# Reordered splits, forms and late T forms in a pooling-mixer and SwiGLU kernel on one core

## What is computed

```python
h = concat(meta, x)                        # 16 + 2048 rows
u = h @ w_in                               # 4 groups of 256 features
d = trailing_mean(u, window) - u           # windows 2, 4, 8, 16, one per group
y = (d @ w_group) * scale                  # 256 x 256 per group
h = layer_norm(ALPHA * h + y @ w_out, g1, b1)
gate, up = split(h @ w_gu)                 # 2816 features each
h = layer_norm(ALPHA * h + (silu(gate) * up) @ w_down, g2, b2)
out = h[16:]
```

## Time and profile before

| | us |
|---|---|
| median of 3 runs (lowest, highest) | 1678.73 (1674.95, 1679.14) |
| the profiled execution | 1677.85 |
| its span | 1676.1 |
| TensorE busy | 1648.3 |
| VectorE busy | 1056.1 |
| GpSimd busy | 707.4 |
| ScalarE busy | 616.5 |

### The profile page before, as it was taken

How to read it: one execution, slowest core, us unless ns; L and a number is a source line. 1 busy time by engine, 2 the same in 40 slices (tenths; PEclk the granted TensorE clock), 3 DMA queues, 4 the chain that set the end, 5 groups by cost and what they waited for, 6 DMA issues and landing times.

```text
span 1676.1 us, 19060 instructions
## 1 busy us (share of the span) xinstructions
PE 1648.3 (98%) x7314; PEld 1360.7 (81%) x7314; DVE 1056.1 (63%) x1069; ACT 616.5 (37%) x836; POOL 707.4 (42%) x455
## 2 busy tenths in 40 slices
PE   9999999999999999999999999999999999999998
PEld 7777888787888888888888887788888888888886
DVE  6679876897444444344757678777654443468866
ACT  5234455355433333434533333333343322232320
POOL 0336125604455566565366777676632000341002
PEclk9999999999999999999999999999999999999999
DMA  9574377544445455466556778775658443554542
GB/s 342 215 273 164 113 262 281 199 162 151 163 151 164 157 195 195 153 226 229 188 181 204 221 245 252 262 219 176 210 179 306 159 156 128 193 211 173 198 149 93
DMA packets 190953, 330.83 MB, mean 197 GB/s; under 512 B 8464, under 2 KB 132496, under 8 KB 181136
## 3 DMA queue, kind: packets, MB, share of 16 engines
q1 hardware_dynamic: 151168, 297.64, 51.4%
q10 hardware_dynamic: 37520, 23.60, 4.7%
q0 software_dynamic: 2176, 8.39, 1.3%
HBM read 227.36 MB, written 102.24 MB: 197 GB/s over the span
## 4 chain that ended last, share of the span: by engine, by line
PE 81%; DVE 5%; POOL 5%; DMA 4%; issue 2%; ACT 1%; SPq 1%; POOLq 0%; DVEq 0%; ACTq 0%
PE acc L1241 37%; PE acc L1270 19%; PE turn L1241 6%; PE turn L1270 6%; PE acc L1108 5%; PE acc L1074 5%; PE turn L1108 3%; DVE sums L1708 2%; DMA wr<-w_gu 1%; POOL ss_mix L871 1%; POOL wt L871 1%; DVE split L1663 1%; DMA hf_dram<-ss_mix 1%; PE acc L1138 1%; POOL dt_t L871 1%
## 5 line engine op out<-in xcount | busy, mean ns | idle before, releaser
L1241 PE MATMUL acc<-fa,wf 128*128 128x512 f32 x1584 | 367.9, 392 | 3.3 <-ACT acc L1586 3.3
L1241 PE MATMUL acc<-fb,wf 128*128 128x512 f32 x1584 | 364.6, 390 | 3.6 <-DVE acc L1930 3.1
L1241 PEld LDWEIGHTS acc<-fb,wf 128*128 128x128 f32 x1584 | 296.8, 188 | 67.6 <-DVE wf L1815 4.0
L1241 PEld LDWEIGHTS acc<-fa,wf 128*128 128x128 f32 x1584 | 297.1, 189 | 65.5 <-issue 4.1
L1270 PE MATMUL acc<-dw,da 128*128 128x512 f32 x1386 | 315.3, 389 | 0.0
L1270 PEld LDWEIGHTS acc<-dw,da 128*128 128x128 f32 x1386 | 260.3, 188 | 53.9
L1815 DVE TENSOR_TENSOR wf<-wt,wf 128x512 fp32r<-128x512 f32 x132 | 136.3, 1037 | 150.7 <-ACT wf L1442 150.2
L1815 DVE TENSOR_TENSOR wf<-wr,wf 128x512 fp32r<-128x512 f32 x176 | 181.8, 1037 | 54.4 <-ACT wf L1442 54.0
L871 POOL TENSOR_TENSOR wt<-wr,wt 128x512 f32<-128x512 f32 x88 | 131.5, 1494 | 163.8 <-DVE wf L1815 163.5
L1074 PE MATMUL acc<-mov,split 128*128 128x512 f32 x768 | 180.4, 394 | 5.8 <-DVE split L1663 5.8
L1442 ACT CAST wf<-wr 128x512 fp32r<-128x512 f32 x176 | 108.7, 618 | 207.9 <-PE acc L1241 205.6
(11 more groups left out here) (136 smaller groups left out, 1963.1 us busy)
## 6 DMA issues: line engine op xcount, KB each, us to landing
wr<-w_gu SPq DMA_DIRECT2D x44, 1024.0 KB, 5.1
dar<-af_dram SPq DMA_DIRECT2D x56, 704.0 KB, 4.2
af_dram<-g ACTq DMA_DIRECT2D x32, 512.0 KB, 6.7
raw<-w_in SPq DMA_DIRECT2D x15, 1024.0 KB, 6.8
fs<-hf_dram SPq DMA_DIRECT2D x14, 1024.0 KB, 5.7
dt_raw<-w_down SPq DMA_DIRECT2D x22, 512.0 KB, 6.5
wt_dram<-dt_t SPq DMA_DIRECT2D x22, 512.0 KB, 4.2
sa<-af_dram SPq DMA_DIRECT2D x22, 512.0 KB, 7.7
```

The lines of the kernel that those rows point to most:

```text
L1241: mm = nc.tensor.matmul(dst, wf[:, slot, a, k, :], fa[half][i][:, v, :, k, :], start=i < 2 and k == 0 and n3 == 0, stop=k == KC - 1 and n3 ...
```

## The change

- Splits of weight chunks (`split_hi`, `split_lo`) move ahead of `stage_u`, `pool` and `rows_stats` in `mixer_block` and `mixer_products`, on both engines.
- Form 2 of h is split one product sooner (t = 3, not 4); form 4's low part and unit 0's first four splits move ahead of the statistics at t = 6; the last form of half 0 moves from place 0 of unit 0 to places 3 (high) and 4 (low). SP's loads of these forms move ahead accordingly, the last one ahead of four stores of rows.
- The five late T forms move from units 26 to 30 to units 38 to 42.
- The load of `gb` moves from unit 33 to step 8 of the down stage (`MT = 8`), and the wait for it to its first use.
- The products with zeros go from 10 to 14.

```diff
--- before.py
+++ after.py
@@ -409,16 +409,17 @@
 
 
 
-        FORM_HI = {(0, 0): NP - 1, (HALF_UNITS - 4, 3): NP, (HALF_UNITS - 2, 3): NP + 1}
+        FORM_HI = {(0, 3): NP - 1, (HALF_UNITS - 4, 3): NP, (HALF_UNITS - 2, 3): NP + 1}
         FORM_HI.update({(HALF_UNITS - 1, place): NP + q for place, q in ((1, 2), (3, 3), (5, 4), (6, 5))})
         FORM_LO = dict(FORM_HI)
+        FORM_LO[0, 4] = FORM_LO.pop((0, 3))
         FORM_HI.update({(HALF_UNITS, 2): NP + 6})
         FORM_LO.update({(HALF_UNITS, 3): NP + 6})
 
 
         TF_STEPS = 2 * JF
         TF_FIRST = tuple(range(3, HALF_UNITS - 2))
-        TF_UNITS = TF_FIRST + tuple(range(HALF_UNITS + 4, HALF_UNITS + 9))
+        TF_UNITS = TF_FIRST + tuple(range(UNITS - 6, UNITS - 1))
         TF_STEP = {n: step for step, n in enumerate(TF_UNITS)}
         assert len(TF_UNITS) == TF_STEPS
 
@@ -767,18 +768,18 @@
             load_form(0)
             load_form(1)
             load_mix(1, 3)
+            load_form(2)
             load_mix(1, 4)
-            load_form(2)
+            load_form(3)
             load_mix(1, 5)
-            load_form(3)
             load_mix(1, 6)
             load_form(4)
             load_unit(0)
             load_form(5)
             load_unit(1)
+            load_form(6)
             for j in range(TT):
                 store_h(2, j)
-            load_form(6)
 
             for n in range(UNITS):
                 half, jj = n // HALF_UNITS, n // 2
@@ -797,10 +798,6 @@
                     store_tform(TF_STEP[n - 1])
                 if n in TF_STEP:
                     load_tform(TF_STEP[n])
-                if n == TF_UNITS[-1] + 3:
-                    sp.wait_ge(tf_stored, 16 * TF_STEPS)
-                    for q, v in enumerate((ffn_g, ffn_b)):
-                        sp.dma_start(gb[:, q, :], v.partition_broadcast(P)).then_inc(gb_landed, 16)
                 if turned_in(n + 1)[1] == 0:
                     load_pair(turned_in(n + 1)[0])
                 if n == TURN0 + 3 * TT:
@@ -844,6 +841,11 @@
                     load_da(k + 3)
                 if k == 2:
                     store_s(JF - 1)
+                if k == MT:
+
+                    sp.wait_ge(tf_stored, 16 * TF_STEPS)
+                    for q, v in enumerate((ffn_g, ffn_b)):
+                        sp.dma_start(gb[:, q, :], v.partition_broadcast(P)).then_inc(gb_landed, 16)
                 if k < 2:
                     load_hz(k + 2)
                 elif 3 <= k < 7:
@@ -1112,7 +1114,7 @@
 
 
             pe.wait_ge(idle_zero, 1)
-            for _ in range(10):
+            for _ in range(14):
                 nc.tensor.matmul(turn[:, 1, :], idle[:, 0:P], idle[:], start=True, stop=True)
 
             def fold_pair_free(q):
@@ -1451,15 +1453,15 @@
 
             def mixer_block(b):
                 for i in range(PAIRS):
+                    c = c_in(b, i) + 1
+                    if c != c_in(0, 1):
+                        split_hi(c, c % 2)
                     if i >= 1:
                         stage_u(b, i - 1)
                     elif b % 2:
                         stage_u(b - 1, PAIRS - 1)
                     if b == 0:
                         stage_meta(i)
-                    c = c_in(b, i) + 1
-                    if c != c_in(0, 1):
-                        split_hi(c, c % 2)
                     if b == 2 and i >= 2:
                         take_turn(i - 2, 2)
                         take_turn(i - 2, 3)
@@ -1485,17 +1487,17 @@
 
             def mixer_products(h):
                 for t in range(NP):
-                    if t == 0:
-                        stage_u(2 * h + 1, PAIRS - 1)
                     c = c_mix(h, t) + 1
                     if c < MIX_END:
                         split_hi(c, c % 2)
+                    if t == 0:
+                        stage_u(2 * h + 1, PAIRS - 1)
                     if 1 <= t < NP - 1:
                         d_hi(h, t + 1)
                     if h == 0 and t in (0, 1, 2, 4):
                         x_hi(2, (0, 1, 2, 4).index(t))
                     if h:
-                        for q in ((), (0,), (1,), (), (2,), (3,), ())[t]:
+                        for q in ((), (0,), (1,), (2,), (), (3,), ())[t]:
                             form_hi(q)
                     if t == 0:
                         for m in range(TT):
@@ -1817,9 +1819,13 @@
 
             def mixer_block(b):
                 for i in range(PAIRS):
+                    c = c_in(b, i) + 1
+                    if c != c_in(0, 1):
+                        split_lo(c, c % 2)
                     if b == 2 and i == 0:
                         rows_stats(0, 6)
                         stats_are_done(1)
+                        aggregate(1)
                     if b == 0 and i >= 1:
                         take_meta(i - 1)
                         dve.wait_ge(meta_u_taken, i)
@@ -1833,11 +1839,6 @@
                         pool(b, i - 1)
                     elif b % 2:
                         pool(b - 1, PAIRS - 1)
-                    c = c_in(b, i) + 1
-                    if c != c_in(0, 1):
-                        split_lo(c, c % 2)
-                    if b == 2 and i == 0:
-                        aggregate(1)
                     if b % 2 and i in (1, 2):
                         d_lo(b // 2, i - 1)
                     if b in (0, 2):
@@ -1845,28 +1846,27 @@
 
             def mixer_products(h):
                 for t in range(NP):
+                    c = c_mix(h, t) + 1
+                    if c < MIX_END:
+                        split_lo(c, c % 2)
                     if t == 0:
                         pool(2 * h + 1, PAIRS - 1)
-                    if t in (2, 5):
+                    if 1 <= t < NP - 1:
+                        d_lo(h, t + 1)
+                    if h and t == NP - 1:
+                        form_lo(4)
+                        for q in range(4):
+                            unit_lo(0, q)
+                    if t in (2, 5, 6):
                         rows_stats(h, t - 1)
-                    if t == 6:
-                        rows_stats(h, 5)
                     if t == 5:
                         stats_are_done(2 * h)
                         aggregate(2 * h)
-                    c = c_mix(h, t) + 1
-                    if c < MIX_END:
-                        split_lo(c, c % 2)
-                    if 1 <= t < NP - 1:
-                        d_lo(h, t + 1)
                     if h == 0 and t in (0, 1, 2, 4):
                         x_lo(2, (0, 1, 2, 4).index(t))
                     if h:
-                        for q in ((), (0,), (1,), (), (2,), (3,), (4,))[t]:
+                        for q in ((), (0,), (1,), (2,), (), (3,), ())[t]:
                             form_lo(q)
-                    if h and t == NP - 1:
-                        for q in range(4):
-                            unit_lo(0, q)
                     if t in (1, 3, 4, 5, 6):
                         add_rows(h, t)
                     if h and t == NP - 1:
@@ -1931,7 +1931,6 @@
                 if n == 0:
                     unit_lo(0, 5)
                     unit_lo(0, 6)
-                    new_form(0, 0)
                 elif nxt:
                     new_form(n, 3)
                     unit_lo(n + 1, 3)
@@ -1991,7 +1990,6 @@
                         down_w_lo(v)
             dve.wait_ge(prod_done, NP * UNITS)
             up_out(2 * JF - 1, 1, bank(UP_LAST, 1))
-            dve.wait_ge(gb_landed, 32)
             dve.wait_ge(normed, BLOCKS * TT)
 
             def take(k):
@@ -2030,6 +2028,8 @@
                 nc.vector.tensor_scalar(var_eps[:, r:r + 1], mv[:, r, 1:2], EPS, None, ALU.add).then_inc(var_ready, 1)
 
             def row_apply(r, zz):
+                if r == 0:
+                    dve.wait_ge(gb_landed, 32)
                 zz = zz.rearrange("p h t -> p (h t)")
                 nc.vector.scalar_tensor_tensor(out=zz, in0=zz, scalar=mv[:, r, 0:1], in1=gb[:, 0, :],
                                                op0=ALU.subtract, op1=ALU.mult).then_inc(centered, 1)
```

## The result

The change makes the kernel slower: 1684.85 us median of five runs (1683.17 to 1687.53) against 1676.52 us of the kernel before in the same session (1674.95 to 1679.14). The ratio is 1.0048, 95% interval [1.0033, 1.0063]. The forecast was 1671. The profiled execution took 1683.17 us with a span of 1681.4, so it is 5.3 us longer by the profiles and 8.3 us by the medians (that of before was 1.3 us over its new median, that of after is the lowest of its five).

What follows compares the result with a forecast made beforehand. TensorE, busy 98% of the span, was taken as the bound, losing only idle and low-clock time. From 1677.85 us, -1.2 - 5.0 - 2.0 - 5.1 + 2.5 - 2.9 - 3.4 + 10 = -7.1 gave 1671, range 1660 to 1678.

Steps and rivals of the forecast that it cites:

- T forms: Late units: leaving units 26 to 30 wins 3.4 us; units 38 to 42 delay w_down's loads, +10 (+2 to +22).
- What is late next: Third product of each half: later pooling delays GpSimd's sums and the form; +1.5 and +1.0, together +2.5 us.
- Warm-up: Kernel start: four more products with zeros raise the clock for the fold; -1.2 us, ends 0 and -2.6.
- Splits first in the blocks: Blocks 0, 1 and 3: splits ahead of staging and pooling remove TensorE's waits; -5.0, -2.0 and -5.1 us.
- The second rival: Blocks to third products: VectorE's equal work swallows the front's gain, 5 of 12.1 us left, near 1677; chance 0.15.
- Statistics behind the split, last form behind the seed: End of half 1 and unit 0: later statistics cost, the seed's wait goes; -2.9 us, ends -4.1 and 0.
- The +0.8 for unit 0: Unit 0: later aggregate delays GpSimd's weight forms and the first units' splits; +0.8 us, ends 0 and 3.
- The late chain: Unit 42 to first down step: last T form's stores and loads hold SP's queue, stored 40.0 us after unit start.
- The slower rival: First down step: SP's queue starves w_down's loads by more, +22 to +26 us, time about 1684; chance 0.13.

Runs made afterwards that it cites:

- the last form alone: Kernel before with only the last form of h cast and split behind unit 0's seed, its load ahead of four stores; 1673.39 us, ratio 0.9986.
- the one a unit sooner: Kernel after with its last five T forms in units 37 to 41 instead of 38 to 42; 1679.07 us, ratio 1.0011.
- the best of after: Kernel after with T forms in units 27, 29, 31, 33, 35, statistics again ahead of the products' splits, GpSimd's sums reordered; 1670.02 us, ratio 0.9962.
- the one with odd units: Kernel after with the last five T forms in units 27, 29, 31, 33 and 35 instead of 38 to 42; 1677.70 us, ratio 1.0009.

## Why the prediction was wrong

By TensorE's timeline, the forecast for everything up to unit 1 was -13.7 us and the trace shows -2.2; for the T forms it was +6.6 and the trace shows +7.5. The step that failed is "What is late next": the loss at the third products, put at +2.5, is +12.7.

**Warm-up:** the meta products start 1.35 us sooner, forecast 1.2. It isn't shown that the warm-up did it: profiles with ten products have them between 30.55 and 32.50 (five), those with fourteen between 30.38 and 31.59 (nine). The two spreads overlap, so no gain of the warm-up can be told; the profile of before was merely the latest of its five. The prediction also read a low clock from the pace of the fold's matmuls. But the granted clock of the kernel before is 1.00 over the whole fold (8 to 32 us), so what slowed its first matmuls stays open. Of the fourteen profiles one has a low stretch there: 0.50 from 10 to 12 us, with the last form alone, ten products with zeros. The prediction named the Trainium skill (TensorE: Matmul & The Clock Gate, Part 1) for a larger gain, 2.6; no run here shows that either.

**Splits first in the blocks:** right. TensorE reaches the products 8.5 us sooner in half 0 and gains 5.5 more in block 3, with 13.3 forecast in all for these and the warm-up.

**What is late next:** put at +2.5, ends 0 and +5; it is +12.7, 6.7 in half 0 and 6.0 in half 1. The mechanism named was the right one (the low part of the third form, behind GpSimd's sums). The size came from a replay in which the last pooling would be early by nearly as much as TensorE. It isn't: the last d is there at 143.48, where the earlier trace rows give 145.34, 1.9 us sooner, while TensorE is 8.5 us sooner. VectorE is why. Its share (third busy column) in the kernel before, two stretches, and in the kernel after:

```profile
116.00:132.00 16.00, 14.13 (x61) 11.42 (x62) 15.86 (x10) 7.37 (x5) 7.67 (x2) 1.00 0.48 175
132.00:150.00 18.00, 18.00 (x81) 14.90 (x80) 16.02 (x12) 5.33 (x6) 12.31 (x4) 1.00 0.51 195
```

```profile
116.00:132.00 16.00, 15.48 (x69) 12.49 (x68) 15.83 (x12) 3.87 (x3) 5.84 (x2) 1.00 0.45 173
```

It was busy for 15.86 of 16 us before the change already, and in the kernel after for 15.83, then for 17.90 of 18; in block 3 for 30.69 of 31 from 278 to 309 (29.39 before). Putting the split first made nothing shorter; it moved the wait to the next thing that VectorE owed. VectorE's timeline of the kernel after has the last d and the low part of the third form:

```profile
140.04 3.44 DVE L1701 TENSOR_TENSOR d<-stage 128x1024 f32<-128x1024 f32 x1
...
155.45 2.68 DVE L1718 TENSOR_TENSOR ring<-d,ring 128x2048 fp32r<-128x2048 f32 x1 [4.21 <-ACT ring L1343]
```

The form is there at 158.13, 14.7 us behind the last d (16.6 before). So it comes 3.8 us sooner, where the replay had 5.9 to 8.0, and TensorE, 8.5 us sooner, waits the 4.7 between. The second rival said this. I gave it 0.15 and counted against it idle stretches of VectorE in blocks 0 and 1; they lie before 116 us (9.73 busy of 16 from 100 to 116, 15.16 in the kernel after), not in the stretch that counts. The two waits of over 3.9 us also cost 2.1 and 1.7 us of low clock.

Operations of 2.2 us that take 4.5 are part of this stretch in both kernels: VectorE's splits of 2.28 take 4.48 or 4.49 where they meet GpSimd's sums. The Trainium skill (SBUF — State Buffer, section "SBUF: two separate sides") calls the port of the two an exclusive lock held for the whole instruction; the rows agree. The prediction drew from it that +5 is nearer than 0, which was the right side but not far enough.

**Statistics behind the split, last form behind the seed:** forecast -2.9, measured -0.8 (1.4 ahead at the fourth product of half 1, 2.2 ahead in unit 1). The wait of the last product is 1.64 (1.7 forecast), the seed's wait is gone. The +0.8 for unit 0 was mis-sized: its first product waits 2.85 us for the row sums. In VectorE's queue they now stand behind the statistics too, and behind unit 0's four weight splits, which take 6.9 us where they took 3.6, beside GpSimd's forms that come later. The forecast had the later GpSimd, not the row sums. Its upper end, 3, holds the wait; with the two orders put back it is gone.

**T forms:** units 26 to 30 gave back what was forecast. The late chain is right link by link: the last T form is stored 39.7 us behind unit 42's start (1204.4), forecast 40.0; w_down's load follows at 41.9, forecast 41; from there to TensorE it takes 8.1, forecast 7.3. The down stage lasts 8.9 us longer and unit 42 waits 3.0, which the forecast left out. Forecast for all this was +10.

**The slower rival** (22 us or more from SP's queue) is not what happened. The kernel ended on the slow side by another way: the front's gains given back, and a T-form loss of the forecast size on top. The second rival had that, but at 1677, since it left 5 us of the 12 won by the splits; 1.4 were left. (By the prediction's own terms, 5 left of 12 gives 1675.4, not 1677.) Even the sum over the trace, +5.3, is under the median's +8.3; I take the 3 us between for scatter of single executions, since the profiled one is the lowest of its five.

## What to carry over

When a wait is removed by reordering one engine's queue, ask whether that engine had idle time between the old and the new place; if it is busy through, the wait only moves, and a wait in a new place can cost more than the old one through the clock. Work put late into a queue that is strictly in order must be counted up to its last store, since the next stage's loads stand behind it. Here taking the late forms out of the units just ahead of that stage was worth 0.3 to 0.4%; whether they stood in full or in light units of GpSimd made no difference that can be told.

## What the runs showed besides

Three of the fourteen profiles (the kernel with late T forms alone, the one a unit sooner, the best of after) have a wait of TensorE in block 3 or right behind it that the others lack, of 5.4 to 6.6 us. VectorE's timeline, block 3, of the best of after and then of the one with odd units:

```profile
282.79 0.18 DVE L1698 COPY stage<-hist 128x32 f32<-128x32 f32 x1 [5.15 <-POOL ss_mix L873]
```

```profile
279.14 0.17 DVE L1698 COPY stage<-hist 128x32 f32<-128x32 f32 x1
```

In all three, pooling waits for GpSimd's sums of the h forms (5.15, 5.15 and 13.08 us), whose third round starts 14.1 to 18.3 us behind the second, and 10.6 to 12.4 in the eleven others. The kernel before has such a wait of pooling too, of 7.63 us, and TensorE waits there for 1.02 and 2.76. The edits don't touch these sums. What makes that round late was not settled, nor how many of the other executions have it. It may be why a profile's span and a median disagree by a few us here, and it is a reason to take the parts of a change this small from the medians of many executions, and from stretches of a trace behind block 3.
